# Retention by chunks of 128 tokens with carried 64x64 states, in place of all pairs of tokens with decay strips

## The chip, the cores and the metric

The kernel runs on one core of a Trainium2 chip. The metric is the device time of one execution in microseconds (us), the median of several.

## The reference

The model is two layers of a transformer block over 512 latent tokens (`x`) and 256 context tokens (`ctx`), width 1024, in fp32. Each layer has a gated feed-forward part, a token mixer and a second gated feed-forward part, each behind a modulated norm. The mixer joins three things: a Fourier transform over positions and features, a retention in both directions with 4 heads of 64, and a windowed attention with 8 query heads and 2 key heads. In layer 1 the context's outputs aren't needed. The retention, which the change rewrites, is:

```python
def retention_scan(q, k, v, log_gamma, state0):   # chunks of 128 tokens
    scores = jnp.einsum('nbhik,nbhjk->nbhij', qc, kc) * intra_decay
    intra = jnp.einsum('nbhij,nbhjv->nbhiv', scores, vc)
    kv = jnp.einsum('nbhjk,hj,nbhjv->nbhkv', kc, k_decay, vc)
    def step(state, kv_chunk):
        return state * chunk_decay[None, :, None, None] + kv_chunk, state
    state_final, state_in = lax.scan(step, state0, kv)
    cross = jnp.einsum('nbhik,nbhkv->nbhiv', qc, state_in) * q_decay[None, None, :, :, None]
    out = (intra + cross).transpose(1, 0, 3, 2, 4).reshape(b, l, h, dv)
    return out, state_final
```

It is called for both directions, first over the context and then, from the context's last state, over the latent tokens; the outputs of the two directions are added, normed by head over 64 values and multiplied by a gate.

## The kernel before

The program is written out engine by engine; each engine runs its own list of instructions in order, and semaphores tie them together. There is no planner. Activations are kept with features on the partitions and the 768 tokens (512 latent, then 256 context) along the free dimension, so a tile of 128 features is 128x768. The big products are done in three passes of fp32r (`split_product`, L623: high by high, high by low, low by high).

In the mixer (`mix` of each engine) the 16 projected tiles stand in `z`. TensorE first does the feature side of the Fourier transform (L761), then its position side (L774, L777) into `pn` and `pg[0]`; ScalarE and VectorE copy the results out as `xhi` (L1156) and `xlo` (L1485). Then come the transposes (L785, L787): each of six blocks of 128 tokens gives 256 columns of retention values (`vret`) and 128 of attention values (`vatt`), copied by VectorE (L1527, L1528).

Then comes the retention, all pairs of tokens in 24 steps, one for each head and block `jt` of 128 keys. `scores` (L809, L810) multiplies a 128-partition stack of high and low keys with two 128-partition stacks of queries, all queries at once: 512 columns, and 256 more where the keys are context and the layer needs the context's output. The stacks are cast by ScalarE (`ret_hi`, L1100 to L1102) and their low parts subtracted by GpSimd (L587). VectorE multiplies the scores with a window of the head's decay strip (L1561, L1563); `values` (L829, L832) multiplies them with `vret` in fp32 and accumulates over the six key blocks in `pg[0]` (heads 0, 1) or `p67` (heads 2, 3). The score tiles alternate between `pg[1]` and `pn`. The four strips, 128x1536 each, are computed by VectorE (L1494, L1500, L1506, L1507) and ScalarE (L1146 to L1149): two of them under the position transform, two between the score steps.

When a pair of heads is done ScalarE squares the result (`squares`, L1119), TensorE averages it over 64 partitions (`variance`, L819), ScalarE makes the reciprocal root (`ret_rstd`, L1125, L1126) and VectorE norms and gates it (`ret_post`, L1535 to L1542). `variance(0)` stands between score steps 14 and 15. Behind `ret_rstd(0)` ScalarE casts the first attention queries (`att_queries_hi`, L1115), and GpSimd subtracts their low parts (L587), after those of the keys. The first attention scores (`att_scores(0)`, L852) wait for these low parts, for `ret_post(0)` and for the last value step, since `pg[0]` is taken over from the retention. The attention runs in units of one block of queries, with scores (L852 to L858), transposes of the probabilities (L883) and values (L899). The output projection and the next feed-forward part follow.

## Time and profile before

| | |
|---|---|
| median of 3 runs | 2834.96 us (2833.14 to 2834.98) |
| profiled execution: its own time, its span | 2828.34 us, 2826.2 us |
| TensorE busy | 2752.1 us, 97% of the span |
| VectorE, ScalarE, GpSimd busy | 1567.6, 715.6, 86.1 us |
| mean granted TensorE clock | 0.992 |
| retention of layer 0, with the transposes ahead of it | 778.2 to 831.9 us |
| the same of layer 1 | 2274.1 to 2321.3 us |

A granted clock of 1.00 is 2.4 GHz, and 0.50 is 1.2 GHz. "Busy" of an engine is the time in which at least one of its instructions ran. The profiled execution is 6.6 us below the median.

### The profile page before, as it was taken

To read this page: it belongs to the slowest core of one execution; us is meant where nothing else is said; L and a number is where in the kernel's file an instruction comes from. 1 tells how busy PE (TensorE), PEld (TensorE's weight loads), DVE (VectorE), ACT (ScalarE), POOL (GpSimd) and SP (SyncE) were. 2 spreads that over 40 slices of the span, in tenths; PEclk is the share of its full clock that TensorE was granted. 3 is DMA by queue.
4 is the path that set the end of the run, shared out by engine and by line. 5 is a ranking of instruction groups with operands and counts; after the bars stand their busy time and mean duration, and the time that the engine had idled before them with its cause. 6 is when DMAs were issued, how large, how long until landed. Compare 5 with 4: busy or idle time off the path is not lost.

```text
span 2826.2 us, 41817 instructions
## 1 busy us (share of the span) xinstructions
PE 2752.1 (97%) x15315; PEld 2330.4 (82%) x15315; DVE 1567.6 (55%) x2711; ACT 715.6 (25%) x1083; POOL 86.1 (3%) x55
## 2 busy tenths in 40 slices
PE   6999999999999999999999999999999999999998
PEld 4888888888749878888888888888887839888887
DVE  6776477453468477725773677257535467533342
ACT  4111111132347231111111311111113346422222
POOL 0000000000131000000000000000000040000000
PEclk9999999999999999999999999999999999999999
DMA  7877577323100157626761576267423300233332
GB/s 230 193 185 172 124 185 185 97 60 85 52 0 2 45 132 185 163 64 162 185 165 58 121 186 170 59 163 185 107 66 90 82 1 2 75 96 104 89 105 88
DMA packets 485787, 319.28 MB, mean 113 GB/s; under 512 B 30588, under 2 KB 481488, under 8 KB 485712
## 3 DMA queue, kind: packets, MB, share of 16 engines
q1 hardware_dynamic: 485712, 318.29, 43.9%
q8 instruction: 45, 0.74, 0.1%
q14 instruction: 30, 0.25, 0.0%
HBM read 316.14 MB, written 2.10 MB: 113 GB/s over the span
## 4 chain that ended last, share of the span: by engine, by line
PE 92%; DVE 3%; ACT 2%; issue 1%; SPq 1%; DMA 1%; DVEq 0%; ACTq 0%
PE pg L623 77%; PE pg L690 4%; PE p L899 2%; PE pn L883 1%; DVE xlo L1437 1%; PE pg L829 1%; PE p L829 1%; PE p L638 1%; DVE tnorm L1429 1%; PE pg L852 1%; PE pn L774 1%; PE pg L774 0%; SPq L521 0%; ACT whi L991 0%; DVE wlo L1291 0%
## 5 line engine op out<-in xcount | busy, mean ns | idle before, releaser
L623 PE MATMUL pg<-xhi,whi 128*128 128x512 f32 x2880 | 802.1, 347 | 8.1 <-DVE wlo L1291 6.0
L623 PE MATMUL pg<-xhi,wlo 128*128 128x512 f32 x2880 | 796.4, 345 | 0.0
L623 PE MATMUL pg<-xlo,whi 128*128 128x512 f32 x2880 | 795.4, 344 | 0.0
L991 ACT CAST whi<-raw 128x1024 fp32r<-128x1024 f32 (+1 forms) x288 | 321.8, 1118 | 1071.4 <-PE pg L623 1063.2
L1291 DVE TENSOR_TENSOR wlo<-raw,whi 128x1024 fp32r<-128x1024 f32 (+1 forms) x288 | 377.5, 1311 | 350.1 <-ACT whi L991 347.2
L623 PEld LDWEIGHTS pg<-xhi,whi 128*128 128x128 f32 x2880 | 455.5, 188 | 77.2 <-DVE wlo L1291 7.5
L623 PEld LDWEIGHTS pg<-xlo,whi 128*128 128x128 f32 x2880 | 454.9, 188 | 70.1
L623 PEld LDWEIGHTS pg<-xhi,wlo 128*128 128x128 f32 x2880 | 454.7, 188 | 69.6
L1370 DVE SCALAR_TENSOR_TENSOR part<-ada,cond,part 128x256 f32<-128x256 f32 x960 | 465.1, 484 | 32.7
L1478 DVE SCALAR_TENSOR_TENSOR h<-pg,gcol,h 128x512 f32 (+1 forms) x118 | 71.3, 638 | 451.3 <-PE pg L623 451.3
L623 PE MATMUL pg<-ahi,whi 128*128 128x512 f32 x1100 | 307.2, 347 | 0.0
L623 PE MATMUL pg<-ahi,wlo 128*128 128x512 f32 x1100 | 304.9, 345 | 0.0
L623 PE MATMUL pg<-alo,whi 128*128 128x512 f32 x1100 | 304.6, 345 | 0.0
L1222 ACT ACTIVATE gate<-pg 128x768 f32<-128x768 f32 (+1 forms) x88 | 66.8, 759 | 576.1 <-PE pg L623 575.0
L623 PEld LDWEIGHTS pg<-alo,whi 128*128 128x128 f32 x1100 | 174.6, 188 | 28.3
L623 PEld LDWEIGHTS pg<-ahi,wlo 128*128 128x128 f32 x1100 | 173.3, 188 | 27.3
L623 PEld LDWEIGHTS pg<-ahi,whi 128*128 128x128 f32 x1100 | 173.9, 188 | 26.4
L1641 DVE TENSOR_TENSOR gate<-gate,pg 128x768 f32<-128x768 f32 (+1 forms) x88 | 78.0, 887 | 137.9 <-PE pg L623 137.9
L690 PE MATMUL pg<-xhi,whi 128*128 128x256 f32 (+1 forms) x240 | 86.1, 359 | 10.5 <-DVE xlo L1437 7.1
L1646 DVE TENSOR_TENSOR alo<-gate,ahi 128x768 f32 (+3 forms) x88 | 78.5, 892 | 9.7
L587 POOL TENSOR_TENSOR rk_st<-z,rk_st 64x768 fp32r<-64x768 f32 x8 | 16.8, 2103 | 2175.9 <-ACT rq_hi L1102 2175.7
L690 PE MATMUL pg<-xlo,whi 128*128 128x256 f32 (+1 forms) x240 | 81.4, 339 | 0.0
(199 smaller groups left out, 2241.0 us busy)
## 6 DMA issues: line engine op xcount, KB each, us to landing
ada<-in_w_ada SPq DMA_DIRECT2D x512, 256.0 KB, 4.1
raw<-in_ffn_w_in SPq DMA_DIRECT2D x176, 512.0 KB, 3.9
raw<-in_ffn_w_out SPq DMA_DIRECT2D x64, 704.0 KB, 4.6
raw<-in_w_in SPq DMA_DIRECT2D x24, 512.0 KB, 3.9
ada_first<-in_w_ada SPq DMA_DIRECT2D x8, 1024.0 KB, 11.8
dft_sb<-in_dft SPq DMA_DIRECT2D x2, 2048.0 KB, 9.1
raw<-in_w_in SPq DMA_DIRECT2D x16, 256.0 KB, 3.6
raw<-in_w_o SPq DMA_DIRECT2D x16, 256.0 KB, 2.8
```

Source lines behind the costliest of these rows:

```text
L623: last = nc.tensor.matmul(pg[s][:, p0:p1], w[:, s, k], v[:, k, p0:p1], start=(k == 0 and n == 0), stop=(k == kt - 1 and n == 2))
L638: last = nc.tensor.matmul(pa[1][:, 2 * b:2 * b + 2], part[:, b * P:(b + 1) * P], halves, start=True, stop=True)
L690: last = nc.tensor.matmul(pg[s][:, c0:c0 + p1 - p0], w[:, s, k], v[:, k, p0:p1], start=(k == 0 and n == 0), stop=(k == kt - 1 and n == 2))
L829: last = nc.tensor.matmul(o[p0:p0 + HD, 0:SEQ], w, sdec[:, r % 2, 0:SEQ], start=(jt == 0), stop=(jt == ret_blocks - 1))
L899: last = nc.tensor.matmul(pa[q // 2 % 2][:, s * HD:(s + 1) * HD], probT[:, q % 2, j * P:(j + 1) * P], vatt[:, kt, s * HD:(s + 1) * HD], st ...
L991: nc.scalar.copy(whi[:, s, 0:nk], raw[:, s, 0:nk]).then_inc(s_whi[s], 1)
L1222: nc.scalar.activation(gate[:, 0:t], pg[0][:, 0:t], ACT.Silu).then_inc(s_free[0], 1)
L1291: nc.vector.tensor_sub(wlo[:, s, 0:nk], raw[:, s, 0:nk], whi[:, s, 0:nk].bitcast(f32)).then_inc(s_w[s], 1)
L1370: ins = nc.vector.scalar_tensor_tensor(part[:, :], ada[q][:, a], cond2[:, n:n + 1], part[:, :], ALU.mult, ALU.add)
L1478: last = nc.vector.scalar_tensor_tensor(hv, pg[s][:, p0:p1], gcol[:, col, v:v + 1].rearrange("p o v -> p (o v)"), hv, ALU.mult, ALU.add)
L1641: nc.vector.tensor_tensor(gate[:, 0:t], gate[:, 0:t], pg[1][:, 0:t], ALU.mult).then_inc(s_free[1], 1)
L1646: nc.vector.tensor_sub(lo, gate[:, 0:t], hi.bitcast(f32)).then_inc(s_a[m, hf], 1)
```

## The change

The retention keeps pairs of tokens only within a chunk of 128 tokens. What lies outside a chunk comes through a state for each head and direction, 64x64, carried from chunk to chunk. The two directions stand one above the other: the forward state on partitions 0 to 63, the backward one on 64 to 127, so that one product with contraction 128 gives both.

- **Transposes** (`block_transposes`, in the order 4, 5, 0, 3, 1, 2): the keys are transposed as well, 256 columns of `z` a block. VectorE copies the values (256 columns) and makes `kdk`, the keys of four heads with the decay of both directions, 512 columns, in one multiply (`block_copies`). The attention's values get one batch of six transposes (`value_transposes`), copied by ScalarE.
- **Chunk products and states**: `chunk_kv` gives the 64x64 products of four heads for the next chunk of either direction, 8 fp32 products with 64 columns, five times a layer. `next_state` on VectorE multiplies the last state with the decay of a chunk and adds the product. GpSimd copies each state to the chunk that it enters (`cross`).
- **Turns**: a turn is a pair of heads and one chunk, 12 turns in layer 0 and 8 in layer 1. `scores` makes two 128x128 score tiles in fp32 straight from `z`, with contraction 64, in the two banks of `pg[1]`, the only score tile. `decayed` multiplies both by the table `dec` (128x128 a head) on VectorE. `values` makes for each head one product of the scores with `vret` and one of the state in `cross` with the decayed queries `qd`.
- **Tables and queries**: the strips, the high and low stacks of keys and queries and their GpSimd parts are gone. ScalarE copies each head's queries to both halves of the partitions and VectorE multiplies them by their decay, under the position transform, where the tables `dec`, `kdec`, `qdt` and `sdk` are made too.
- **Order**: `variance(0)` stands behind turn 7 in layer 0 and turn 5 in layer 1, and `ret_post(0)` behind the last two `decayed`. A row of query positions and two columns of key positions join the constants; the distance table shrinks from 896 to 128 columns.

```diff
+        xlo0 = start["xlo"]
+        kdk = place("kdk", [P, TOK // P, RH, 2, HD], f32, xlo0 + 4 * TOK * 4)
+        qd = [place(f"qd{hd}", [P, TOK], f32, x0 + k * TOK * 4) for hd, k in enumerate((2, 3, 6, 7))]
+        qdt = place("qdt", [P, RH, P], f32, start["ada"] + 2 * TOK * 4)
+        cross = place("cross", [P, TOK // P, RH * HD], f32, m0 + 2 * TOK * 4)
+        state = place("state", [P, 5, RH * HD], f32, t0 + 3072)
+        stmp = place("stmp", [P, RH * HD], f32, t0 + 3072 + 5120)
...
+        turn_order = [4, 5, 0, 3, 1, 2]
+        fwd, bwd = [4, 5, 0, 1, 2, 3], [5, 4, 3, 2, 1, 0]
+        def ret_turns(l):
+            order = [4, 5, 1, 2, 0, 3] if l < DEPTH - 1 else [1, 2, 0, 3]
+            return [(p, tt) for p in range(RH // 2) for tt in order]
+        def cross_count(l, tt):
+            step = max(fwd.index(tt), bwd.index(tt))
+            return 2 * step if l < DEPTH - 1 else 2 * (step - 1)
...
+                for s in range(5):
+                    pool.wait_ge(s_st[l], s + 1)
+                    for own, tt in ((slice(0, HD), fwd[s + 1]), (slice(HD, P), bwd[s + 1])):
+                        if tt * P < tq:
+                            nc.gpsimd.tensor_copy(cross[own, tt], state[own, s]).then_inc(s_cr[l], 1)
...
+                def block_transposes(a):
+                    tt = turn_order[a]
+                    if a >= 2:
+                        pe.wait_ge(s_v[l], a - 1)
                     for v in range(2):
-                        nc.tensor.matmul(pa[tt % 2][:, v * P:(v + 1) * P], z[:, RV_T + v, tt * P:(tt + 1) * P],
+                        nc.tensor.matmul(pa[a % 2][:, v * P:(v + 1) * P], z[:, RV_T + v, tt * P:(tt + 1) * P],
                                          center, start=True, stop=True)
-                    nc.tensor.transpose(pa[tt % 2][:, 2 * P:3 * P], z[:, AV_T, tt * P:(tt + 1) * P], ident
-                                        ).then_inc(s_vt[l], 1)
-                pe.wait_ge(s_v[l], ret_blocks)
-                pe.wait_ge(s_y[l], 2)
-                spare = [pg[1], pn]
-                def free_slot(turn):
-                    what, r = ret_turns[turn - 2]
-                    pe.wait_ge(s_sd[l] if what == "scores" else s_rr[l], r + 1)
...
+                def value_transposes():
+                    pe.wait_ge(s_y[l], 1)
+                    for tt in range(ret_blocks):
+                        last = nc.tensor.transpose(pn[:, tt * P:(tt + 1) * P], z[:, AV_T, tt * P:(tt + 1) * P], ident)
+                    last.then_inc(s_avt, 1)
+                def chunk_kv(s):
+                    pe.wait_ge(s_v[l], max(turn_order.index(fwd[s]), turn_order.index(bwd[s])) + 1)
+                    if s == 0:
+                        pe.wait_ge(s_va, l + 1)
+                    else:
+                        pe.wait_ge(s_st[l], s - 1)
+                    for dr, tt in enumerate((fwd[s], bwd[s])):
+                        for hd in range(RH):
+                            at = s % 2 * 512 + hd * HD
+                            last = nc.tensor.matmul(pn[HD * dr:HD * dr + HD, at:at + HD], kdk[:, tt, hd, dr],
+                                                    vret[:, tt, hd * HD:(hd + 1) * HD], start=True, stop=True)
+                    last.then_inc(s_kv[l], 1)
+                turns = ret_turns(l)
+                def scores(r):
+                    p, tt = turns[r]
+                    if r:
+                        pe.wait_ge(s_sd[l], r)
+                    for b in range(2):
+                        own, at = slice(HD * b, HD * b + HD), 512 * b
+                        last = nc.tensor.matmul(pg[1][:, at:at + P], z[own, RK_T + p, tt * P:(tt + 1) * P],
+                                                z[own, RQ_T + p, tt * P:(tt + 1) * P], start=True, stop=True)
                     last.then_inc(s_s[l], 1)
-                def variance(turn, p):
-                    free_slot(turn)
+                def values(r):
+                    p, tt = turns[r]
+                    pe.wait_ge(s_sd[l], r + 1)
+                    pe.wait_ge(s_qd[l], 2 * p + 2)
+                    pe.wait_ge(s_cr[l], cross_count(l, tt))
+                    for b in range(2):
+                        hd = 2 * p + b
+                        o = (pg[0], p67)[p][HD * b:HD * b + HD, tt * P:(tt + 1) * P]
+                        nc.tensor.matmul(o, vret[:, tt, hd * HD:(hd + 1) * HD], sdec[r % 4][:, b],
+                                         start=True, stop=False)
+                        last = nc.tensor.matmul(o, cross[:, tt, hd * HD:(hd + 1) * HD],
+                                                qd[hd][:, tt * P:(tt + 1) * P], start=False, stop=True)
+                    last.then_inc(s_pv[l], 1)
+                def variance(p):
                     pe.wait_ge(s_osq[l], p + 1)
+                    if p:
+                        pe.wait_ge(s_rr[l], p)
                     for p0, p1 in [(0, SEQ)] + ([(SEQ, TOK)] if tq == TOK else []):
-                        last = nc.tensor.matmul(spare[turn % 2][:, p0:p1], block, osq[:, p, p0:p1],
-                                                start=True, stop=True)
+                        last = nc.tensor.matmul(pn[:, p0:p1], block, osq[:, p, p0:p1], start=True, stop=True)
                     last.then_inc(s_var[l], 1)
-                def values(r):
-                    hd, jt = ret_steps[r]
-                    p0 = HD * (hd % 2)
-                    pe.wait_ge(s_sd[l], r + 1)
...
+                for a in range(ret_blocks):
+                    block_transposes(a)
+                    if a == 1:
+                        value_transposes()
+                    if 2 <= a < 4:
+                        chunk_kv(a - 2)
+                chunk_kv(2)
+                scores(0)
+                chunk_kv(3)
+                chunk_kv(4)
+                pe.wait_ge(s_y[l], 2)
+                for r in range(len(turns)):
+                    if r + 1 < len(turns):
+                        scores(r + 1)
+                    values(r)
+                    if r == nt + 1:
+                        pe.wait_ge(s_st[l], 5)
+                        variance(0)
+                pe.wait_ge(s_y[l], 3)
+                pe.wait_ge(s_kl[l], 2 * KV_HEADS)
+                att_scores(0)
+                variance(1)
...
+                def query_copies(hd):
                     b = hd % 2
-                    own, oth = slice(HD * b, HD * b + HD), slice(HD - HD * b, 2 * HD - HD * b)
-                    k, q = z[own, RK_T + hd // 2, :], z[own, RQ_T + hd // 2, 0:tq]
-                    if hd >= 2:
-                        act.wait_ge(s_s[l], ret_blocks * (hd - 1))
-                    nc.scalar.copy(rk_st[b][own, :], k)
-                    nc.scalar.copy(rq_hi[b][own, 0:tq], q)
-                    nc.scalar.copy(rq_hi[b][oth, 0:tq], q).then_inc(s_rh[l], 1)
+                    for half in range(2):
+                        last = nc.scalar.copy(qd[hd][HD * half:HD * half + HD, 0:tq],
+                                              z[HD * b:HD * b + HD, RQ_T + hd // 2, 0:tq])
...
+                for dr in range(2):
+                    b = (2 * l + dr) * RH
+                    nc.scalar.activation(kdec[:, :, dr], lg[:, b:b + RH], ACT.Exp, scale=kpos[:, dr:dr + 1])
+                nc.scalar.activation(sdk[:, :], lgq[:, l], ACT.Exp, scale=float(P)).then_inc(s_kd, 1)
+                for hd in range(RH):
+                    nc.scalar.activation(qdt[:, hd], qpos, ACT.Exp, scale=lgq[:, l, hd:hd + 1])
+                query_copies(0)
+                act.wait_ge(s_da, l + 1)
+                nc.scalar.activation(dec[:, :, :], dec[:, :, :], ACT.Exp).then_inc(s_de, 1)
+                for hd in range(1, RH):
+                    query_copies(hd)
...
+                act.wait_ge(s_avt, l + 1)
+                nc.scalar.copy(vatt[:, 0:4].rearrange("p a b -> p (a b)"), pn[:, 0:SEQ])
+                nc.scalar.copy(vatt[:, 4:6].rearrange("p a b -> p (a b)"), pn[:, SEQ:TOK]).then_inc(s_va, 1)
+                act.wait_ge(s_vt[l], ret_blocks)
...
+                def decay_args():
+                    for hd in range(RH):
+                        b = (2 * l + 1) * RH + hd
+                        done = mark(nc.vector.tensor_scalar(dec[:, hd], dist_sb[:, :], nlg[:, b:b + 1], None, ALU.mult))
+                    dve.wait_ge(s_dv, done)
+                    for hd in range(RH):
+                        b = 2 * l * RH + hd
+                        last = nc.vector.scalar_tensor_tensor(dec[:, hd], dist_sb[:, :], lg[:, b:b + 1], dec[:, hd],
+                                                              ALU.mult, ALU.min)
+                    last.then_inc(s_da, 1)
+                def query_decay(hd):
+                    dve.wait_ge(s_qc[l], hd + 1)
+                    q = qd[hd][:, 0:tq].rearrange("p (c t) -> p c t", t=P)
+                    nc.vector.tensor_tensor(q, q, qdt[:, hd].unsqueeze(1).broadcast_to([P, nt, P]), ALU.mult
...
+                    dve.wait_ge(s_de, l + 1)
+                    nc.vector.tensor_tensor(dec[:, :, :], dec[:, :, :],
+                                            ident.unsqueeze(1).broadcast_to([P, RH, P]), ALU.add).then_inc(s_dr, 1)
+                def block_copies(a):
+                    tt = turn_order[a]
+                    dve.wait_ge(s_vt[l], a + 1)
+                    nc.vector.tensor_copy(vret[:, tt], pa[a % 2][:, 0:256])
+                    if a == 0:
+                        dve.wait_ge(s_kd, l + 1)
+                    kT = pa[a % 2][:, 256:512].rearrange("p (h d) -> p h d", h=RH)
+                    nc.vector.tensor_tensor(kdk[:, tt], kT.unsqueeze(2).broadcast_to([P, RH, 2, HD]),
+                                            kdec[:, :, :].unsqueeze(3).broadcast_to([P, RH, 2, HD]), ALU.mult
+                                            ).then_inc(s_v[l], 1)
+                def next_state(s):
+                    new = state[:, s]
+                    kv = pn[:, s % 2 * 512:s % 2 * 512 + 256]
+                    if s:
+                        dve.wait_ge(s_st[l], s)
+                        old = state[:, s - 1].rearrange("p (h d) -> p h d", h=RH)
+                        link(nc.vector.tensor_tensor(stmp[:, :].rearrange("p (h d) -> p h d", h=RH), old,
+                                                     sdk[:, :].unsqueeze(2).broadcast_to([P, RH, HD]), ALU.mult))
+                    dve.wait_ge(s_kv[l], s + 1)
+                    if s:
+                        nc.vector.tensor_tensor(new, kv, stmp[:, :], ALU.add).then_inc(s_st[l], 1)
+                    else:
+                        nc.vector.tensor_copy(new, kv).then_inc(s_st[l], 1)
+                turns = ret_turns(l)
+                def decayed(r):
+                    p, tt = turns[r]
+                    dve.wait_ge(s_s[l], r + 1)
+                    if r >= 4:
+                        dve.wait_ge(s_pv[l], r - 3)
+                    src = pg[1][:, :].rearrange("p (b c) -> p b c", b=2)[:, :, 0:P]
+                    nc.vector.tensor_tensor(sdec[r % 4][:, :, :], src, dec[:, 2 * p:2 * p + 2], ALU.mult
+                                            ).then_inc(s_sd[l], 1)
...
+                for a in range(3):
+                    block_copies(a)
+                next_state(0)
+                block_copies(3)
+                next_state(1)
+                block_copies(4)
+                block_copies(5)
+                next_state(2)
+                dve.wait_ge(s_dr, l + 1)
+                decayed(0)
+                next_state(3)
+                next_state(4)
+                for r in range(1, len(turns)):
+                    decayed(r)
+                    if r >= len(turns) - 2:
+                        for stage in range(2):
+                            ret_post(0, 2 * (r - len(turns) + 2) + stage)
```

## Rows read from the trace of the kernel before

**Rows 1.** The page's chain that ended last, by line, shares of the span.
```profile
PE pg L623 77%; PE pg L690 4%; PE p L899 2%; PE pn L883 1%; DVE xlo L1437 1%; PE pg L829 1%; PE p L829 1%; PE p L638 1%; DVE tnorm L1429 1%; PE pg L852 1%; PE pn L774 1%; PE pg L774 0%; SPq L521 0%; ACT whi L991 0%; DVE wlo L1291 0%
```

**Rows 2.** Stage table: stretch, length, each engine's busy us, clock, DMA share, GB/s.
```profile
761.00:778.00 17.00, 17.00 (x48) 8.77 (x48) 10.90 (x9) 9.13 (x12) 13.55 (x6) 1.00 0.00 1
778.20:831.90 53.70, 50.63 (x163) 21.07 (x161) 33.05 (x57) 18.17 (x22) 22.48 (x12) 1.00 0.00 0
838.00:841.00 3.00, 3.00 (x13) 2.79 (x13) 2.90 (x6) 0.43 (x3) 0.00 (x0) 0.50 0.00 0
848.00:925.00 77.00, 75.32 (x649) 73.51 (x648) 61.56 (x202) 55.09 (x187) 7.24 (x4) 1.00 0.01 2
```

**Rows 3.** TensorE's timeline, layer 0: start, length, line, tiles, count [idle before].
```profile
778.21 0.61 PE L785 MATMUL p<-consts,z 128*128 128x128 f32 x4
778.65 0.27 PE L787 MATMUL p<-consts,z 128*128 128x128 f32 x1
778.76 0.61 PE L785 MATMUL p<-consts,z 128*128 128x128 f32 x4
...
784.40 0.50 PE L809 MATMUL pg<-rq_hi,rk_st 128*128 128x512 f32 x1 [0.71 <-DVE vatt L1528]
...
792.78 0.28 PE L809 MATMUL pn<-rq_hi,rk_st 128*128 128x256 f32 x1
792.90 0.28 PE L810 MATMUL pn<-rq_lo,rk_st 128*128 128x256 f32 x1
793.11 1.07 PE L829 MATMUL pg<-sdec,vret 128*64 128x512 f32 x2
794.02 0.59 PE L832 MATMUL pg<-sdec,vret 128*64 128x256 f32 x2
794.54 0.50 PE L809 MATMUL pg<-rq_hi,rk_st 128*128 128x512 f32 x1
...
811.36 1.56 PE L819 MATMUL pn<-osq,consts 128*128 128x512 f32 x4
...
831.91 0.39 PE L852 MATMUL pg<-ak_hi,aq_st 128*128 128x256 f32 x1
```

**Rows 4.** TensorE's timeline, layer 1.
```profile
2274.05 0.61 PE L785 MATMUL p<-consts,z 128*128 128x128 f32 x4
...
2304.53 1.12 PE L819 MATMUL pn<-osq,consts 128*128 128x512 f32 x2
...
2321.33 0.38 PE L852 MATMUL pg<-ak_hi,aq_st 128*128 128x256 f32 x1
```

**Rows 5.** TensorE's timeline, the first modulation, 46 to 49 us.
```profile
46.98 1.92 PE L665 MATMUL p<-ada_first,cond 128*32 128x512 f32 x16
```

**Rows 6.** VectorE's timeline, layer 0.
```profile
780.11 0.41 DVE L1527 COPY vret<-p 128x256 f32<-128x256 f32 x1
...
791.32 0.42 DVE L1561 TENSOR_TENSOR sdec<-pg,strips 128x256 f32<-128x256 f32 x1
791.66 0.68 DVE L1563 TENSOR_TENSOR sdec<-pg,strips 128x512 f32<-128x512 f32 x1
...
795.97 1.68 DVE L1506 TENSOR_TENSOR strips<-strips,consts 128x128 f32<-128x128 f32 x1
```

**Rows 7.** ScalarE's timeline, the first query casts of either layer.
```profile
814.63 1.67 ACT L1115 CAST aq_st<-z 64x768 fp32r<-64x768 f32 x2
...
2306.95 1.24 ACT L1115 CAST aq_st<-z 64x512 fp32r<-64x512 f32 x2
```

**Rows 8.** GpSimd's timeline.
```profile
795.70 1.81 POOL L587 TENSOR_TENSOR rk_st<-z,rk_st 64x768 fp32r<-64x768 f32 x1 [19.79 <-ACT rq_hi L1102]
...
820.33 3.71 POOL L587 TENSOR_TENSOR aq_st<-z,aq_st 64x768 fp32r<-64x768 f32 x2
...
2312.81 2.61 POOL L587 TENSOR_TENSOR aq_st<-z,aq_st 64x512 fp32r<-64x512 f32 x2
```

**Rows 9.** Groups by line, the attention's values: records, busy us, mean ns, idle before.
```profile
L899 PE MATMUL p<-vatt,probT 128*128 128x64 f32 x640 | 80.3, 269 | 0.0
```

189 lines of the change are left out of this document (46 added, 143 removed).

## The prediction

> **What bounds the kernel now.** I read the chain of waits first, then a table by stages, then the timelines of TensorE, VectorE, ScalarE and GpSimd around the retention of each layer. The chain [rows 1] is almost all TensorE; the big products of the feed-forward and projection phases (L623) hold 77% of it, and the diff doesn't touch them. The retention's own value products (L829) hold 2%. In the stage table [rows 2] the retention of layer 0 with the transposes ahead of it, 778.2 to 831.9 us, keeps TensorE busy for 50.6 of 53.7 us, at a granted clock of 1.00 (2.4 GHz), and no transfer runs there. So TensorE sets the length of this stretch, and what its instructions cost there is what the change can save, once for each layer. From the end of the position transform to the first attention scores it is 778.21 to 831.91 us, 53.7 us, in layer 0 [rows 3], and 2274.05 to 2321.33 us, 47.3 us, in layer 1 [rows 4]. What lies before 778.21 is bound by the transform's own products, and what lies behind 831.91 is the same code in both kernels. I forecast the start of `att_scores(0)` in each layer, and carry the shift to the end unchanged, since after it only TensorE-bound phases follow.
>
> **Prices on TensorE.** An fp32 product leaves two records. Two of them with 128 columns and 128x128 weights take 778.65 - 778.21 = 0.44 us, so 0.22 each, and a transpose 0.11 [rows 3]. A 512-column product with 64-wide weights takes 0.91 us; the 256-column one behind it takes 0.52 up to the next product with full-width weights, against 0.455 as half of 0.91, so going back to another shape of the array costs 0.07; going into it costs 0.09 (792.90 to 793.11 is 0.21, where the like product from 792.78 to 792.90 took 0.12) [rows 3].
>
> **The head: transposes, chunk products, states.** The diff removes the strips, the high and low stacks of queries and keys, and 48 (24 a layer) score-value steps with 512 or 768 columns. Before the transform ends it adds, on VectorE and ScalarE, the 128-wide decay tables, the copies of the queries and their decay, in place of two strips and six stack casts. Those fit: 10.9 us of VectorE and 9.1 us of ScalarE were busy in the 17 us under the transform [rows 2], and by my count the new ones are about 7 us and 9 us (four 768-wide multiplies on VectorE at about 0.9, and small ones; eight 64x768 copies on ScalarE at 0.83, half of the 1.67 pair [rows 7], the 768-wide cast and small ones). Nothing on that side costs; if the cover were gone, it would be 2 us at most. Under it GpSimd is now idle.
>
> Behind the transform the walk for layer 0 is this. TensorE does block 0 and 1 at 0.44 + 2 x 0.11 = 0.66 each and six attention transposes (0.66), until 780.2. VectorE can't begin its copies before the old `xlo` step is through, which is when it began them in the trace, 780.11 [rows 6]. A `block_copies` is a 256-column copy (0.41, of which 0.08 overlap with the next, 791.32 to 791.66 against 0.42) and a 512-column multiply (0.68), so 0.33 + 0.60 = 0.93 us of VectorE, and six of them 5.6 us. A `chunk_kv` is 8 products with 64-wide weights and 64 columns, 16 records. The trace has no such shape. From below, a record can't beat half of 0.11, so 16 x 0.055 = 0.9 us; from above, the attention's 64-column products with full weights take 80.3 us for 640 records, 0.125 each, so 2.0 us [rows 9]. I take 1.2, nearer the lower one because the weights have half the columns. The order on TensorE then gives: block 2 waits for copies 0 (781.15) and ends at 781.9; chunk 0 waits for copies 1 (782.1) and ends at 783.3; block 3, chunk 1, blocks 4 and 5, chunk 2 follow to 787.7; scores(0) to 788.2, chunk 3 to 789.4, chunk 4 to 790.6. VectorE runs in step with it: copies 3 from 784.1, 4 from 785.95, 5 from 786.9, and the states between. The state update is a 256-column multiply in SBUF and a 256-column add out of PSUM (0.42), and is late for nobody until the last two, behind which `decayed(1)` is queued. Here GpSimd counts: it copies each state into `cross`, and a VectorE step with its inputs in SBUF that met a GpSimd step took 1.68 us at 795.97 while GpSimd ran from 795.70 to 797.51 [rows 6, 8]. A GpSimd step of 64x768 is 1.81 us, so a 64x256 copy is 0.4 to 0.8; I charge 0.6 us for one such meeting. The turns begin in effect at 791.2, 13.0 us behind the transform, where the old scores began 6.2 us behind it (784.40) [rows 3]. The head thus costs 6.8 us more than before.
>
> The Trainium skill, "SBUF — State Buffer", states that GpSimd holds the port pair that it shares with VectorE for a whole instruction, and that a VectorE instruction with two SBUF inputs then blocks. Row 795.97 agrees; by the page each of the four state multiplies could be held for a whole copy, some 2 us a layer in place of 0.6.
>
> **The turns.** A turn is now two score products (128 columns, contraction over 64) and four value products (64-wide weights, 128 columns): 6 x 0.22 + 0.09 + 0.07 = 1.48 us if they go one behind the other. TensorE has 0.88 us of value products to do while VectorE decays the next scores (0.42 and some 0.2 for the two hand-overs), so although `pg[1]` is the only score tile, VectorE is hidden. I take t = 1.45, between this and the value for side-by-side products below. From above it is 12 records x 0.125 + 0.16 = 1.66 [rows 9].
>
> The last turn isn't what the attention waits for. `variance(0)` follows values 7 in layer 0 and values 5 in layer 1; from its start to the end of the two query casts the old trace has 816.30 - 811.36 = 4.94 us, and 2308.19 - 2304.53 = 3.66 us [rows 3, 4, 7]. GpSimd's two low parts then end 3.71 - 0.83 = 2.9 us later (2.61 - 0.62 = 2.0 in layer 1) [rows 7, 8], since the first starts after the first cast. So `att_scores(0)` starts at 791.2 + 8 x 1.45 + 7.8 = 810.6 in layer 0. TensorE itself is through at 791.2 + 11 x 1.45 + 0.95 + 1.2 = 809.3, and `ret_post(0)`, which stands ahead of and behind the last `decayed` on VectorE and meets GpSimd's low parts, may add a little: I take 811.2. The saving is 831.91 - 811.2 = 20.7 us. In layer 1 the head is 0.4 us shorter (its `xlo` step is 512 wide), so turns begin at 2286.7, and the attention at 2286.7 + 6 x 1.45 + 5.7 + 0.5 = 2301.6: 19.7 us saved. Behind it the same waits follow, the low-clock stretch of 838 to 841 too [rows 2].
>
> At the start the constants grow by 130 columns and the distance table shrinks by 768; two small multiplies become four small copies under the loads. I set that at nothing, within 0.5 us.
>
> **Sum.** 20.7 + 19.7 = 40.4 us. The profiled execution is 2826.2 us of span in 2828.3 us; it would become 2787.9. The median shown is 6.6 us above it, so 2834.96 - 40.4 = 2794.6, and I say 2795.
>
> **Rivals.**
> *A, products side by side.* The 512-column products of the start, 8 of them with 32-wide weights, take 1.92 us [rows 5], where one behind the other they would take 8 x 0.91 = 7.3. So products in different column groups overlap here. The two score products of a turn lie in different row halves and write different banks; if they overlap, 0.2 go, and 0.1 where the second head's values begin in the other column half: t = 1.2. With chunks at 0.9 the sum is 14 x 0.25 + 2 x 1.5 = 6.5 us less, 2788. Against it: within a head, and in four products in a row of a chunk, the group is the same.
> The Trainium skill, "TensorEngine Tiling (Array Packing)", Key Properties, says that tiles work independently but that a change of tiling mode drains the array, and this kernel changes it twice a turn. The 0.07 and 0.09 us are what the trace shows of that.
> *B, small products at the pace of their weight loads.* At 0.125 a record, chunks take 2.0 and turns 1.66: 2 x 4 + 14 x 0.2 = 11 us more, 2806. For it: the 640 narrow attention products do run so [rows 9]. The full hold by GpSimd would land here too.
> *C, the other side: the array at half clock.* From 838 to 841 the granted clock was 0.50 (1.2 GHz), behind the wait at the attention's start [rows 2]. If the small products and waits held it there through both stretches, TensorE's 11 us of work in a head would become 22, the turns of layer 0 would end at 11 x 2.9 + 4.3 = 36 us after their start in place of 20, and those of layer 1 24 in place of 14.9: 22 + 16 + 9 = 47 us more, 2842, slower by 0.25%. It decides from about 85% of the stretches at the low clock. Against it, 649 small products and transposes in 848 to 925 us kept 1.00 [rows 2].
> The Trainium skill, "TensorE: Matmul & The Clock Gate", Part 4, says that transposes don't count as busy for the clock; the head has 18 of them where 6 stood. The attention's stretch, where transposes stand in every unit, doesn't show it.
> *D, the change doesn't pay.* A chain not seen gives all back, 2835.
>
> **Chances.** The forecast 0.45, A 0.24, B 0.25, C 0.03, D 0.03. The main case alone spans 2789 to 2801. The range reaches from the lower bounds (2788, less 2 for a shorter tail) to B with a fallen clock for one short stretch: 2786 to 2808. A measurement of this kernel can tell about 0.2% (5.7 us) from no change; faster than that 0.93, within it 0.03, slower 0.04.
>
> **What would show it.** The first attention scores at about 811 and 2302 us; turns 1.45 us apart in TensorE's timeline; chunks of 1.2 us; a head of 13 us that TensorE fills to 85%; VectorE idle between `decayed` steps; `att_scores(0)` released by GpSimd's `aq_st` and not by the values. The prediction is wrong if turns are over 1.9 us apart, if scores wait for VectorE in each turn, if the head takes over 16 us, or if the granted clock in it is under 1.00.

## The result and the profile after

The changed kernel takes 2792.4 us (median of 4 executions, 2790.8 to 2795.6), beside 2835.0 us for the kernel before in the same session: a ratio of 0.9849, with a 95% interval of 0.9837 to 0.9862. The prediction said 2795 us, with 2786 to 2808 as its range. The profiled execution took 2790.8 us, its span is 2788.6 us, 37.6 us below the span of before.

The chain that ended last, by line, in the changed kernel. L641 and L708 are the old L623 and L690 [rows 1]; L829 and L855 are now the chunk and value products, and neither is in the list any more.
```profile
PE pg L641 79%; PE pg L708 4%; PE p L943 2%; PE pn L927 1%; PE p L656 1%; DVE xlo L1468 1%; PE pg L886 1%; DVE tnorm L1460 1%; PE pn L792 1%; PE pg L792 0%; ACT whi L1035 0%; PE pg L891 0%; DMA ada_first<-in_w_ada 0%; DVE wlo L1320 0%; PE pg L892 0%
```

TensorE's timeline of the changed kernel, layer 0, from the end of the position transform (779.50) to the first attention scores (809.29). It answers to [rows 3].
```profile
779.50 0.61 PE L805 MATMUL p<-consts,z 128*128 128x128 f32 x4
...
783.40 0.97 PE L829 MATMUL pn<-vret,kdk 128*64 128x64 f32 x16
784.29 0.71 PE L805 MATMUL p<-consts,z 128*128 128x128 f32 x4
...
790.77 0.49 PE L842 MATMUL pg<-z 64*128 64x128 f32 x4
...
793.27 0.49 PE L842 MATMUL pg<-z 64*128 64x128 f32 x4
793.69 0.45 PE L855 MATMUL pg<-sdec,vret 128*64 128x128 f32 x4
...
794.29 0.49 PE L842 MATMUL pg<-z 64*128 64x128 f32 x4
...
799.38 1.56 PE L867 MATMUL pn<-osq,consts 128*128 128x512 f32 x4
...
806.67 0.70 PE L855 MATMUL p<-sdec,vret 128*64 128x128 f32 x4 [2.69 <-DVE sdec L1583]
...
809.29 0.58 PE L886 MATMUL pg<-ak_hi,aq_st 128*128 128x256 f32 x1 [1.49 <-DVE xlo L1610]
```
The stretch, from the first transposes to the first attention scores, is 29.79 us long where it was 53.70. A chunk is 784.29 - 783.40 = 0.89 us, a turn 794.29 - 793.27 = 1.02 us. Ahead of the last turn's values TensorE stands still for 2.69 us, and ahead of the attention for 1.49 us, and both times VectorE releases it. Layer 1, in the same view, goes from 2255.78 to 2280.84, 25.06 us where it was 47.28 [rows 4], with the same two waits:
```profile
2255.78 0.61 PE L805 MATMUL p<-consts,z 128*128 128x128 f32 x4
...
2273.75 1.12 PE L867 MATMUL pn<-osq,consts 128*128 128x512 f32 x2
...
2279.16 0.45 PE L855 MATMUL p<-sdec,vret 128*64 128x128 f32 x4 [3.27 <-DVE sdec L1583]
...
2280.84 0.58 PE L886 MATMUL pg<-ak_hi,aq_st 128*128 128x256 f32 x1 [1.01 <-DVE xlo L1610]
```
VectorE's timeline in layer 0 shows what it did in those waits: `ret_post(0)` from 802.78, with the last decay (806.19) in its middle; from 815.75 on, the like steps of `ret_post(1)`.
```profile
790.00 0.48 DVE L1566 TENSOR_TENSOR stmp<-state,sdk 128x256 f32<-128x256 f32 x1
...
803.78 2.38 DVE L1605 SCALAR_TENSOR_TENSOR osq<-osq,vecs,z 128x768 f32<-128x768 f32 x1
806.19 0.42 DVE L1583 TENSOR_TENSOR sdec<-pg,dec 128x256 f32<-128x256 f32 x1
806.54 1.71 DVE L1608 CAST xhi<-osq 128x768 fp32r<-128x768 f32 x1
808.28 0.96 DVE L1610 TENSOR_TENSOR xlo<-osq,xhi 128x768 fp32r<-128x768 f32 x1
...
815.75 1.02 DVE L1605 SCALAR_TENSOR_TENSOR osq<-osq,vecs,z 128x768 f32<-128x768 f32 x1
816.80 0.56 DVE L1608 CAST xhi<-osq 128x768 fp32r<-128x768 f32 x1
```
GpSimd's timeline, layer 0:
```profile
789.82 0.93 POOL L616 COPY cross<-state 64x256 f32<-64x256 f32 x2 [1.83 <-DVE state L1570]
...
803.55 4.28 POOL L604 TENSOR_TENSOR aq_st<-z,aq_st 64x768 fp32r<-64x768 f32 x2 [2.97 <-ACT aq_st L1154]
```
The same two VectorE steps took 2.38 and 1.71 us while GpSimd ran (803.55 to 807.83), and 1.02 and 0.56 us while it did not: 2.5 us on a path that TensorE waits for.

Windows of the changed kernel, with the columns of [rows 2]:
```profile
779.50:790.77 11.27, 10.38 (x128) 9.09 (x126) 9.61 (x21) 4.68 (x7) 3.08 (x8) 1.00 0.01 1
804.00:808.00 4.00, 1.13 (x8) 0.73 (x8) 3.97 (x3) 0.47 (x2) 3.75 (x2) 0.70 0.00 0
808.00:812.00 4.00, 2.71 (x7) 1.90 (x8) 2.11 (x4) 0.67 (x1) 0.00 (x0) 0.50 0.00 0
```
The head keeps 1.00. The clock falls during the 2.69 us wait, to 0.50 (1.2 GHz), and the attention begins at that level.

**Where the 37.6 us are.** The two stretches give 23.91 + 22.22 = 46.1 us. Outside them the profiled execution is 8.5 us longer: 1.3 before the transform ends (779.50 against 778.21), 1.2 in the attention of layer 0 (100.9 us from its first scores to the output projection, against 99.8), 1.9 in that of layer 1 (79.8 against 77.9), 3.2 between that projection and layer 1's projection phase (1326.1 against 1323.0), and 1.0 at the end (428.0 against 427.0). A second profile of the same kernel, further down, tells which parts of this stay.

### The profile page after: what moved, and what is told of

Read it like the earlier page. It is cut to its first block, busy times and chain, and to the rows that moved or that the text cites. A ratio compares the mean times of both kernels' runs of the same rounds, so it can differ in the third digit from the quotient of the medians.

```text
span 2788.6 us, 42172 instructions
## 1 busy us (share of the span) xinstructions
PE 2709.2 (97%) x15515; PEld 2332.8 (84%) x15515; DVE 1536.4 (55%) x2689; ACT 695.9 (25%) x1071; POOL 49.2 (2%) x51
## 4 chain that ended last, share of the span: by engine, by line
PE 92%; DVE 4%; ACT 2%; issue 1%; DMA 1%; SPq 1%; DVEq 0%; ACTq 0%
PE pg L641 79%; PE pg L708 4%; PE p L943 2%; PE pn L927 1%; PE p L656 1%; DVE xlo L1468 1%; PE pg L886 1%; DVE tnorm L1460 1%; PE pn L792 1%; PE pg L792 0%; ACT whi L1035 0%; PE pg L891 0%; DMA ada_first<-in_w_ada 0%; DVE wlo L1320 0%; PE pg L892 0%
## 5 line engine op out<-in xcount | busy, mean ns | idle before, releaser
L641 PE MATMUL pg<-xhi,whi 128*128 128x512 f32 x2880 | 804.0, 347 | 8.0 <-DVE wlo L1320 6.0
L641 PE MATMUL pg<-xhi,wlo 128*128 128x512 f32 x2880 | 797.5, 345 | 0.0
L641 PE MATMUL pg<-xlo,whi 128*128 128x512 f32 x2880 | 796.4, 345 | 0.0
L641 PEld LDWEIGHTS pg<-xhi,whi 128*128 128x128 f32 x2880 | 455.8, 188 | 77.4 <-DVE wlo L1320 7.5
L641 PEld LDWEIGHTS pg<-xlo,whi 128*128 128x128 f32 x2880 | 456.2, 188 | 71.4
L641 PEld LDWEIGHTS pg<-xhi,wlo 128*128 128x128 f32 x2880 | 455.3, 188 | 70.0
L641 PE MATMUL pg<-ahi,whi 128*128 128x512 f32 x1100 | 306.4, 347 | 0.0
L641 PE MATMUL pg<-ahi,wlo 128*128 128x512 f32 x1100 | 305.8, 346 | 0.0
L641 PE MATMUL pg<-alo,whi 128*128 128x512 f32 x1100 | 305.6, 346 | 0.0
L641 PEld LDWEIGHTS pg<-alo,whi 128*128 128x128 f32 x1100 | 174.2, 188 | 27.5
L641 PEld LDWEIGHTS pg<-ahi,whi 128*128 128x128 f32 x1100 | 174.3, 188 | 27.3
L641 PEld LDWEIGHTS pg<-ahi,wlo 128*128 128x128 f32 x1100 | 174.0, 188 | 27.4
L708 PE MATMUL pg<-xhi,whi 128*128 128x256 f32 (+1 forms) x240 | 85.9, 358 | 10.8 <-DVE xlo L1468 7.4
L708 PE MATMUL pg<-xlo,whi 128*128 128x256 f32 (+1 forms) x240 | 81.2, 338 | 0.0
L708 PE MATMUL pg<-xhi,wlo 128*128 128x256 f32 (+1 forms) x240 | 81.0, 337 | 0.0
```

Of the source, the lines that this page charges most:

```text
L641: last = nc.tensor.matmul(pg[s][:, p0:p1], w[:, s, k], v[:, k, p0:p1], start=(k == 0 and n == 0), stop=(k == kt - 1 and n == 2))
L708: last = nc.tensor.matmul(pg[s][:, c0:c0 + p1 - p0], w[:, s, k], v[:, k, p0:p1], start=(k == 0 and n == 0), stop=(k == kt - 1 and n == 2))
```

## The experiments

All ran beside the kernel before: 2833.1 us for the first four, 2834.4 us for the last four (7 executions each). Line numbers past an edit move by a few.

**Two score tiles.** What sets the 1.02 us of a turn: TensorE's own products, or the round trip TensorE, VectorE, TensorE through the one score tile? The odd scores from turn 3 on go to `pn`, free by then.
```
+def score_tile(l, r):
...
+    return pn if r % 2 and 3 <= r <= nt + 1 else pg[1]
...
-    if r: pe.wait_ge(s_sd[l], r)
...
+    before = [a for a in range(r) if score_tile(l, a) is tile]
+    if before: pe.wait_ge(s_sd[l], before[-1] + 1)
```


> The changed kernel with a second score tile: the odd turns from 3 up to the one before variance(0) write their scores to pn, so scores(r+1) no longer waits for decayed(r) there. Turns are 1.02 us apart in the changed kernel. If the round trip over VectorE (0.54 us from the score products to the start of decayed, 0.42 for it, 0.06 back) sets the turn, turns 3 to 7 of layer 0 fall under 0.95 us. If TensorE's own products set it (0.42 for the scores and 0.60 for the values stand without a gap in its timeline), they stay at 1.02 within 0.03. In time either is under 1.5 us, so only the timeline decides; the ratio to the kernel before stays at 0.984 to 0.986.

It took 2793.7 us (2791.5 to 2794.9), ratio 0.986 [0.984, 0.988]. TensorE's timeline, first record of three turns:
```profile
794.26 0.49 PE L851 MATMUL pn<-z 64*128 64x128 f32 x4
...
795.27 0.49 PE L851 MATMUL pg<-z 64*128 64x128 f32 x4
...
796.29 0.49 PE L851 MATMUL pn<-z 64*128 64x128 f32 x4
```
Turns stay at 1.02 us with twice the room. The round trip is hidden; TensorE's products are the turn.

**Interleaved halves.** On top of it, products of different halves of the array alternate: in a chunk the two directions, in a turn the two heads.
```
-for dr, tt in enumerate((fwd[s], bwd[s])):
-    for hd in range(RH):
+for hd in range(RH):
+    for dr, tt in enumerate((fwd[s], bwd[s])):
...
-for b in range(2):   # values b, then cross b
+for part_ in range(2):
+    for b in range(2):   # both values, then both crosses
```


> As e1_two_tiles, and the products alternate between the two column halves of the array: in values first both heads' score-value products, then both state products; in chunk_kv forward and backward take turns for each head. If products in different column halves run side by side, a chunk of 16 records falls from 0.89 us to 0.45 to 0.65, the value part of a turn from 0.60 to 0.35 to 0.45, and the run is 2 to 5 us shorter than e1_two_tiles. If they don't, chunk and value part stay as they are within 0.05 us and the time is that of e1_two_tiles.

It took 2793.6 us (2784.6 to 2795.8), ratio 0.9856 [0.9828, 0.9883]. TensorE's timeline, a chunk and a turn:
```profile
785.78 0.69 PE L834 MATMUL pn<-vret,kdk 128*64 128x64 f32 x16
786.40 0.71 PE L810 MATMUL p<-consts,z 128*128 128x128 f32 x4
...
795.33 0.49 PE L851 MATMUL pn<-z 64*128 64x128 f32 x4
795.76 0.44 PE L867 MATMUL pg<-sdec,vret 128*64 128x128 f32 x4
...
796.34 0.49 PE L851 MATMUL pg<-z 64*128 64x128 f32 x4
```
A chunk falls from 0.89 to 0.62 us, a turn only from 1.02 to 1.01: the value part stays at 0.58, where 0.35 to 0.45 was expected, and the time is that of two score tiles, where 2 to 5 us less was expected. In the chunks four products in a row had used one half, and the overlap came with the new order; in a turn the old order already had it, as the run with the same halves shows below. The head gained only 0.4 us in the stretch (29.43), since VectorE's copies, decays and states are back to back there from 787.4 to 793.0.

**Early casts.** The two query casts on ScalarE stand behind `squares(0)` and `ret_rstd(0)`, so GpSimd's low parts begin only as `ret_post(0)` does. They are moved ahead.
```
 att_keys_hi()
+att_queries_hi(0, 0)
+att_queries_hi(0, 1)
 squares(0)
 ret_rstd(0)
-att_queries_hi(0, 0)
-att_queries_hi(0, 1)
```


> The changed kernel with the two casts of the first attention queries moved on ScalarE from behind ret_rstd(0) to behind the key casts, so that GpSimd does their low parts right behind those of the keys, before ret_post(0) begins. If the meeting of ret_post(0) with these low parts is what stretched it (its multiply-multiply step took 2.38 us in layer 0 where the same step of the second pair took 1.02, its cast 1.71 where it took 0.56), these return to 1.0 and 0.6, att_scores(0) starts 1.5 to 2.5 us earlier in each layer, and the run is 3 to 8 us shorter, more if the clock no longer falls there. If the steps are slow for another reason, nothing changes in them and the time stays within 1 us.

It took 2786.5 us (2784.1 to 2791.7), ratio 0.984 [0.9817, 0.9863]. VectorE, GpSimd and TensorE, layer 0, one view each:
```profile
804.67 1.41 DVE L1605 SCALAR_TENSOR_TENSOR osq<-osq,vecs,z 128x768 f32<-128x768 f32 x1
...
806.45 0.55 DVE L1608 CAST xhi<-osq 128x768 fp32r<-128x768 f32 x1
```
```profile
801.56 3.70 POOL L604 TENSOR_TENSOR aq_st<-z,aq_st 64x768 fp32r<-64x768 f32 x2
```
```profile
806.59 0.45 PE L855 MATMUL p<-sdec,vret 128*64 128x128 f32 x4 [1.71 <-DVE sdec L1583]
...
808.05 0.39 PE L886 MATMUL pg<-ak_hi,aq_st 128*128 128x256 f32 x1 [0.80 <-DVE xlo L1610]
```
GpSimd is through at 805.26. The step that still meets it for a part takes 1.41, the one behind takes 0.55; both waits shrink (1.71 and 0.80), the stretch is 27.67 us, and the clock stays at 1.00 from 804 to 828. That the attention waits for VectorE's `ret_post(0)`, stretched by GpSimd, is shown: only ScalarE's two casts moved, and GpSimd's low parts with them, and in the changed kernel those casts had ended (804.32) well before the slow VectorE cast at 806.54 began. Layer 1's stretch fell by 0.4 us only, where 1.5 to 2.5 was expected. Its casts did start early (2263.72), but GpSimd's low parts of the keys stand ahead of those of the queries: they ran from 2265.74 to 2273.21, and the queries' from 2273.28 to 2276.22, still beside `ret_post(0)`. The time alone doesn't separate this run from the changed kernel, since the intervals of their ratios overlap; the timeline does.

**Fillers.** Does keeping TensorE busy in the two waits hold the clock? Products that nobody reads stand in the waits: three ahead of the last values, one ahead of the attention.
```
+if r == len(turns) - 1:   # one more such product stands behind the last turn
+    pe.wait_ge(s_rr[l], 1)
+    for _ in range(3):
+        nc.tensor.matmul(pn[:, P:512], ident, z[:, RK_T, 0:384], start=True, stop=True)
 values(r)
```


> The changed kernel with four idle products (384 columns, fp32, into pn, read by nobody) on TensorE: three ahead of the last turn's values, where it waited 2.7 and 3.3 us, and one ahead of the wait for ret_post(0). If the low granted clock behind this wait (0.63, 0.75 and 0.53 in the three stretches from 804.3 to 819 us of the changed kernel) comes of TensorE's idleness there and costs time, the clock stays at 1.00 from there to the attention and the run is 2 to 6 us shorter. If the fall has another cause, or the waits of the attention's start hide it, the time stays within 1 us or grows by the fillers.

It took 2790.6 us (2784.9 to 2793.8), ratio 0.9845 [0.9822, 0.9868]. Windows, columns as before:
```profile
804.00:811.00 7.00, 5.92 (x46) 3.23 (x40) 6.30 (x7) 3.36 (x5) 4.21 (x2) 1.00 0.00 0
812.00:816.00 4.00, 2.30 (x13) 1.57 (x11) 2.24 (x5) 2.21 (x4) 0.00 (x0) 1.00 0.00 0
816.00:820.00 4.00, 3.23 (x16) 2.93 (x16) 3.86 (x6) 1.61 (x6) 0.00 (x0) 0.70 0.00 0
```
The fall ahead of the attention is gone. In layer 0 it came later, in the attention's own first waits (TensorE busy 2.30 of 4 us), and that attention took 102.8 us, 1.9 more than in this profile of the changed kernel and as much as in its second one (102.9). In layer 1 the clock stayed at 1.00 from 2272 to 2296, and that attention took 77.6 us, 2.1 less than in the changed kernel and as much as before the change (77.9). So filling a wait moved the fall in one layer and removed it in the other, but the time didn't change by more than the interval: inconclusive as a gain.

**Same halves.** Are the products of the two heads side by side? Scores read 64 partitions, so they use one row half of the array; values write 64 partitions, so they use one column half. Here both heads' scores use the first 64 partitions, and both heads' values the first 64 output partitions. The kernel so leaves out the values of heads 1 and 3, and serves for its timeline only.
```
-own, at = slice(HD * b, HD * b + HD), 512 * b
+own, at = slice(0, HD), 512 * b
...
-o = (pg[0], p67)[p][HD * b:HD * b + HD, tt * P:(tt + 1) * P]
+o = (pg[0], p67)[p][0:HD, c:c + P]   # c = tt * P for b 0, TOK for b 1
```


> The changed kernel with both heads of a pair in the same half of the array: the second head's scores are made from the first head's 64 partitions, and its values go to the first head's 64 output partitions, in spare columns. The number and the sizes of the products stay; heads 1 and 3 of the output aren't computed. In the changed kernel a turn is 1.02 us, 0.42 for two score products and the way to the values, 0.60 for four value products. If this is short of my sum of 1.48 because the two heads' products run side by side in different halves, the turn rises to 1.4 to 1.55 us here (scores 0.55 to 0.6, values 0.85 to 0.95). If instead a small fp32 product simply costs less than 0.22 us, whatever its place, the turn stays at 1.02 within 0.05.

One execution, 2800.9 us. TensorE's timeline, one turn:
```profile
795.51 0.71 PE L842 MATMUL pg<-z 64*128 64x128 f32 x4
796.15 0.43 PE L856 MATMUL pg<-sdec,vret 128*64 128x128 f32 x2
796.42 0.38 PE L858 MATMUL pg<-qd,cross 128*64 128x128 f32 x2
796.64 0.38 PE L856 MATMUL pg<-sdec,vret 128*64 128x128 f32 x2
796.85 0.38 PE L858 MATMUL pg<-qd,cross 128*64 128x128 f32 x2
797.17 0.71 PE L842 MATMUL pg<-z 64*128 64x128 f32 x4
```
The same six products take 797.17 - 795.51 = 1.66 us: scores 0.64 in place of 0.42, values 1.02 in place of 0.60. Value products here follow each other by 0.21 to 0.27 us, about the 0.22 us of [rows 3]. The turn is 0.11 us above the range that was expected, and far from the 1.02 us of the rival, that a small product is cheap in any place. In the changed kernel the pairs overlap, which is worth 0.64 us a turn.
The Trainium skill, "TensorEngine Tiling (Array Packing)", Key Properties, says that different tiles of the array work in parallel. This run agrees (1.66 against 1.02 us).

**Late post.** The casts stay early, and VectorE does the last decay first and `ret_post(0)` whole behind it. The attention's first scores then wait only for the step of it that reads their tile.
```
 decayed(r)
-    if r >= len(turns) - 2:
-        for stage in range(2):
-            ret_post(0, 2 * (r - len(turns) + 2) + stage)
+for stage in range(4):
+    ret_post(0, stage)
...
-pe.wait_ge(s_y[l], 3)
+pe.wait_ge(s_rp[l], 1)   # counts the first stage of ret_post
```


> e3_early_casts, and the four steps of ret_post(0) stand behind the last decayed on VectorE, and att_scores(0) waits only for the first of them, the one that reads pg[0], and no longer for xlo. If the waits ahead of att_scores(0) are what VectorE's order and the meeting with GpSimd make, TensorE's 1.7 us wait ahead of the last values goes in layer 0, att_scores(0) starts 2 us earlier than in e3_early_casts, and the clock stays at 1.00 there. In layer 1 GpSimd's low parts of keys and queries, 7.5 and 2.9 us one behind the other, end only about 1 us before att_scores(0) starts in e3_early_casts, so no more than 1 us is to be had there. In time 1 to 4 us under e3_early_casts (2786.5). Rival: VectorE has the same work ahead of the first reduce_max, so the attention's pace is unchanged and the time too.

It took 2784.2 us (2779.6 to 2787.5), ratio 0.9823 [0.98, 0.9847]. TensorE's timeline, either layer's attention:
```profile
809.76 0.39 PE L887 MATMUL pg<-ak_hi,aq_st 128*128 128x256 f32 x1 [0.20 <-DVE osq L1604]
...
2275.26 0.36 PE L887 MATMUL pg<-ak_hi,aq_st 128*128 128x256 f32 x1 [3.05 <-POOL aq_st L605]
```
Layer 0's stretch is 25.29 us, with 0.20 us of the wait left. In layer 1 (23.77 us) GpSimd's low parts are last now, as the prediction had it for both layers. The two stretches are 3.3 us shorter together than with early casts; the medians differ by 2.3 us, and the ranges of their executions overlap.

**All together.** Late post, with interleaved halves (and one score tile, as in the changed kernel), and layer 1's first two low parts on VectorE.
```
+if l == DEPTH - 1:
+    for v in range(KV_HEADS):
+        dve.wait_ge(s_qh[l], v + 1)
...
+        nc.vector.tensor_sub(st[oth, 0:tq], z[own, AQ_T, 0:tq], st[own, 0:tq].bitcast(f32)).then_inc(s_ql[l], 1)
 for stage in range(4):
     ret_post(0, stage)
```


> e6_late_post with the interleaved products of e2_interleaved, and in layer 1 VectorE makes the low parts of the first queries in its idle time ahead of ret_post(0), so that GpSimd's chain no longer sets the start of the attention there. Expected: a head 0.5 us shorter, att_scores(0) of layer 1 another 1.5 to 2.5 us earlier than in e6_late_post, 2779 to 2784 us. Rival: VectorE's two steps lengthen its own chain by 1.4 us and meet GpSimd's key parts, so that nothing is gained in layer 1.

It took 2778.3 us (2774.8 to 2788.1), ratio 0.9802 [0.9781, 0.9823]. The two stretches are 24.97 and 22.33 us; the wait in layer 1 falls from 3.05 to 1.95 us:
```profile
2273.19 0.39 PE L887 MATMUL pg<-ak_hi,aq_st 128*128 128x256 f32 x1 [1.95 <-DVE osq L1604]
```
The profiled execution was the slowest of its four (2788.1 us), and its windows show one place where it loses:
```profile
2276.00:2280.00 4.00, 2.81 (x16) 2.69 (x16) 3.86 (x7) 2.36 (x8) 0.00 (x0) 0.83 0.00 0
2280.00:2284.00 4.00, 3.33 (x15) 3.19 (x15) 2.03 (x6) 2.92 (x8) 1.08 (x1) 0.50 0.00 0
```
The attention of layer 1 took 85.0 us, 5.2 more than in the changed kernel. The two stretches are 7.6 us shorter than in the changed kernel's second profile, and the median is 14.0 us lower; what the other 6.4 us are isn't shown; the pace of the big products (see below) may be a part.

**The changed kernel again.** The same text beside the last three.


> The changed kernel once more, on the chip and beside the runs of these three, as their measure. Expected 2790 to 2796 us, ratio 0.984 to 0.986, a granted clock under 1.00 somewhere between 804 and 820 us of its profile, and att_scores(0) released by VectorE's xlo, 29.8 us and 25.1 us behind the position transform.

It took 2792.3 us (2789.3 to 2795.2), ratio 0.9854 [0.9832, 0.9876]; the stretches are 29.80 and 25.07 us, to 0.01 us those of the first profile. All executions of late post and of all together are faster than its fastest. The interval of late post (up to 0.9847) still overlaps its own; that of all together (up to 0.9823) doesn't.

## Why the prediction was right, step by step

**What bounds it: right, up to the tails.** TensorE set the stretches until their last two waits, where VectorE did, and all but 8.5 us of their shortening reached the end.

**The head: right in kind, 1.7 us too long.** Forecast 13.0 us, measured 11.27 (layer 1: 12.65 and 10.79). The copies cost VectorE 0.33 + 0.60 us, as forecast. A chunk was 0.89, not 1.2: of its bounds the lower was the true one, and the interleaved run shows that even 0.89 is no floor. The 0.6 us for a meeting with GpSimd didn't come: the multiply at 790.00 lies inside GpSimd's copy at 789.82 and took 0.48 us, where its likes take 0.41 to 0.42 (the row holds two copies, and ends 0.27 us after the multiply). TensorE was busy for 10.38 of 11.27 us, 92% in place of 85%.
The Trainium skill, "SBUF — State Buffer", section "Who interferes with whom", would have that multiply wait for the end of the copy that runs. Each copy takes about 0.43 us (0.85 for two), so the first ran to about 790.25, an estimate from these rows, and the multiply would have ended at about 790.66; it ended at 790.48. This row doesn't show the full hold. The 2.38 us row, against a GpSimd subtraction, roughly agrees with it: it is 1.36 us longer than alone, and the subtraction, 1.81 us by [rows 8], had 1.58 us to go when it began.

**The turns: the mis-sized term.** Forecast 1.45 us, "if they go one behind the other"; measured 1.02. Rival A had the mechanism (products in different halves overlap), and took too little from it with 1.2. The experiment with equal halves shows it. From the second scores to the first variance it was 8.61 us in layer 0 for 11.6, and 7.18 in layer 1 (2266.57 to 2273.75) for 8.7. That VectorE stays hidden behind one score tile was right but for the first turns, where TensorE waits for VectorE's decay behind the last states, 0.40 us in layer 0 and 1.00 in layer 1.

**The tail: the wrong releaser.** Forecast 8.4 us from the variance to the attention, released by GpSimd's `aq_st`; measured 9.91, released by VectorE's `xlo` (layer 1: 6.2 and 7.09). The prediction named the cause and charged it 0.6 us: `ret_post(0)` meets GpSimd's low parts. GpSimd was through 8.45 us behind the variance (803.55 + 4.28 against 799.38), near the 7.8 us forecast for it, so its path was priced about right. The meeting cost 2.5 us on the two VectorE steps, and the last `decayed`, queued behind the first of them, held TensorE for 2.69 us. With shorter turns there was also less for TensorE to do in that time. Early casts and late post settle this.

**What was carried unchanged: wrong by 8.5 us between the two profiles, by 3.5 us between the medians.** The forecast of the stretches, 40.4 us, was 5.7 short, and nothing was set aside for what lies outside. So the profiled execution came within 2.9 us of the forecast 2787.9 because two errors cancel, which is luck. The profiled execution of before lies 6.6 us below its median and that of the changed kernel 1.6 below its own, and these 5.0 us are chance of which execution was profiled. The medians are 42.6 us apart, so 3.5 us of the stretches' 46.1 are lost outside (4.0 by the medians beside the second profile). Of the parts, those of the long stretch and ahead of the transform differ about as much or more between two profiles of the changed kernel; the 1.0 us at the end is in all nine profiles of it and its versions (427.9 to 428.3 us), and its cause is open.

The waits ahead of the attention bring the clock down where before it fell only from 836 to 844 us. That is a part of the 1.2 and 1.9 us in the attentions: layer 0's took 99.5 us with early casts, and layer 1's 77.6 us with fillers, both without that fall. How low the clock goes and for how long differs between profiles of the same kernel too (layer 0's attention 100.9 and 102.9 us), and no run settles why.

The long stretch between the output projection of layer 0 and the transform of layer 1 took 1326.1 us in the first profile of the changed kernel and 1323.1 in the second, beside 1323.0 before. At its very start the same products ran at the low clock in one and at the high one in the other, TensorE's timeline, first profile and second:
```profile
911.34 0.79 PE L641 MATMUL pg<-xhi,whi 128*128 128x512 f32 x2
```
```profile
917.17 0.51 PE L641 MATMUL pg<-xhi,whi 128*128 128x512 f32 x2
```
Added up from the granted clocks in windows of 10 us, TensorE spent about 24 us of this stretch at the low level in the first profile, 14 in the second and 17 before. A microsecond there does half the work, so 24 against 17 is worth 3.4 us, an estimate from these sums, and the 3.2 us are of that size. Since the second profile doesn't have them, no run ties them to the change. The nine profiles of the changed kernel and its versions spread over 1322.6 to 1327.0 us.

The big products of layer 0's projection phase, from the first L623 or L641 to the transform, took 117.70 us before and 119.92 after, at the same clock. The rows for the same 30 us, of before, of the changed kernel and of all together:
```profile
670.00:700.00 30.00, 30.00 (x175) 26.24 (x174) 1.00 0.28 65
```
```profile
670.00:700.00 30.00, 30.00 (x172) 26.00 (x171) 1.00 0.28 65
```
```profile
670.00:700.00 30.00, 30.00 (x175) 26.21 (x174) 1.00 0.25 59
```
There are two paces, 171 to 173 records and 175. All together, a version of the changed kernel, has the pace of before, and its phase took 117.70 us too; the other eight profiles took 119.92 to 119.94. Elsewhere one kernel shows both: from 1780 to 1810 us the changed kernel has 172 records in its first profile and 175 in its second, and from 550 to 580 us it is 175 and 172. So the pace isn't a property of the program text alone. That the change makes the slower pace more frequent in this phase (eight profiles of nine, against none of one) isn't excluded, and what sets it is open.

**Rivals B, C, D.** B fell: the turns are at 1.02, chunks at 0.89. C didn't come in the heads and turns, which kept 1.00, but the clock fell at the ends of the stretches. D fell.

## What to carry to other kernels

Price small products by which part of the array they use: neighbours in different halves overlap, and neighbours in the same half queue. The order of the loop can decide it (0.89 to 0.62 us for a chunk), or change nothing (1.02 to 1.01 us for a turn, whose values change halves after every two products anyway). When a TensorE stretch gets shorter, list everything that was hidden under it, with GpSimd's steps beside VectorE's: here the wait moved to a VectorE chain that GpSimd stretched, and moving two casts and one decay made the two stretches 5.8 us shorter and the median 8 us lower (the whole set 7.6 and 14 us). A forecast in the trace's own stretches should set aside some microseconds for what lies outside them, and a difference of a few microseconds there should be looked for in two profiles of the same kernel before it is put down to the change.

## What the runs showed of the hardware

- Two fp32 score products of 128 columns in different row halves take 0.42 us up to the next product, in the same half 0.64. Four value products take 0.60 in two column halves and 1.02 in one.
- Eight products of 64 columns take 0.89 us in blocks of four per half, and 0.62 us alternating.
- A VectorE step met by GpSimd's subtraction was stretched even as a cast with one input (1.71 against 0.56 us), while one met by GpSimd's copy was hardly (0.48 against 0.41).
- The granted clock fell to 0.50 around waits of 2.69 and 1.49 us on TensorE. It stayed at 1.00 when these were 1.71 and 0.80 (early casts, layer 0). With late post only 0.20 us of wait was left ahead of the attention of layer 0, and the clock fell further on, in the attention's own first waits (0.83 from 812 to 816, TensorE busy for 1.87 of 4 us).
- The same products at clock 1.00 ran at 172 or at 175 records in 30 us, in different phases and different executions of one kernel.
